# Bank rotation of the last product, tile order of the next layer's first chunk, and a narrower wait of one left part

## The chip, the cores and the metric

The kernel runs on one core of one Trainium2 chip. The metric is device time in microseconds (us) of one execution; three executions of the kernel before are given with their median, and a fourth was profiled.

## What is computed

Two layers of an encoder over 768 tokens (a prompt of 256 and a sample of 512), model width 2048:

```
for l in range(2):
    h = rms_norm(x) * ln_g[l]
    q, k, v, gates = split(h @ w_in[l])
    mix = concat[A(q, k, v) * silu(g_A), B(...) * silu(g_B), C(...) * silu(g_C)]
    x = x + mix @ w_out[l]
```

A, B and C are three kinds of attention (windowed, dense, dilated), and `mix` is 2048 wide. What matters here is the last line, the product of `mix` with `w_out`, and the first line of layer 1, which follows on it.

## The kernel before, in words

**Numbers.** Every fp32 operand is split in a high and a low part (ACT casts the high one, DVE subtracts to get the low one), and each product is three matmuls: high x high, high x low, low x high. The tokens are 6 tiles of 128 (`TT`).

**Stages of a layer.** Input projection (`project_chunk`, 9 slabs of 16 weight chunks, accumulating in banks 0 to 5, one for each token tile; `norm_turns` transposes x beside it, with `norm_hi_parts` on ACT and `norm_lo_parts` on DVE as the evacuation); attention with the gate projection woven in (`gate_piece`); then the output product.

**The output product.** `mix @ w_out` is made as 7 products of half-sized blocks (`PRODUCTS`, Strassen's scheme: 3 token tiles x 2 column slabs each, so 6 tiles, with sums of weights prepared ahead and sums of left parts made on the way). A product is 8 left parts (`KH`) by 2 column slabs (`NH`), 16 chunks; a chunk (`product_step`, L1452 to L1454) is 3 tiles of 3 matmuls. Chunk e of a layer runs from 0 to 111; chunks 96 to 111 are the last product (number 6). Tile b of product p accumulates in bank `out_bank(p, b)`. When a product ends, DVE adds each tile into x (`add_product`, L2162 or L2164), once for each target in `to`: products 0, 2, 3, 4 and 5 have two targets a tile, product 1 and product 6 one. `ADD_AT` puts the adds of tiles 0, 1, 2 in the program at the product's last chunk, those of tiles 3 and 4 one chunk later, tile 5's two later. Before a tile's first matmul PE waits until the adds of all earlier tiles of that bank are done.

**Left parts.** `a_hi_part` (ACT, L1800) and `a_lo_part` (DVE, L2149) write the left operand for part q into a ring of four places. Parts 0 and 1 are made early; part 2 goes to place 0 and part 3 to place 1. These two places lie over the two slots of `gate_t`, in which the gates are kept (gate n of the layer in slot n % 2), so ACT waits for the count `gated`, which POOL raises twice a gate (`gate_product`, L2319). PE needs part q at chunk 2q.

**Queues.** Each engine works off its program in order. In chunk e's turn ACT splits weight chunk e + 4 (L1629; it waits until chunk e - 1 is used), then casts a left part at even e, then does norm work; DVE does adds, the low split of chunk e + 4 (L1890), a sum of left parts (L2142) or a low part (L2149), then norm work. SP issues the DMAs of weights (L1066), of the last mixed chunk's store (L1172), of x (L1218) and of mixed chunks (L1179), in the order of its own program, the loads of x behind the store's landing.

**The way into layer 1.** `NORM_ENTRY` puts the turns of layer 1's first four norm chunks behind chunks 99, 103, 107 and 111 of layer 0, into banks 6 and 7, which the last product leaves free. Then `project_chunk(1, 0)` takes tiles 0 to 5 in banks 0 to 5, each when that bank's adds are done:

```
return (p * OUT_BANKS + b) % 8 if p < N_PROD - 1 else (b + 4) % 6
NORM_ENTRY = {((N_PROD - 1) * KH + 2 * k + 1) * NH + 1: k for k in range(NORM_EARLY)}
act.wait_ge(gated, 2 * (l + 1) * GATE_TILES)
```

Of the kernel before, what the change touches and what calls it, by code (L numbers as in the profile page):

```python
# [31 lines left out]
ACT = mybir.ActivationFunctionType  # L32
# [3 lines left out]
P = 128  # L36
# [4 lines left out]
TT = TOKENS // P  # L41
# [35 lines left out]
KH = KC // 2  # L77
TH = TT // 2
NH = NS_OUT // 2
# [13 lines left out]
OUT_BANKS = TH * NH  # L93
# [2 lines left out]

def out_bank(p, b):

    return (p * OUT_BANKS + b) % 8 if p < N_PROD - 1 else (b + 4) % 6


def quadrant_slab(quadrant, h):
# [289 lines left out]
A_TMP = 3  # L392
A_LEAD = 2

A_EARLY = 2
EARLY_TURN = BIAS_LAST[-1] + 12
NORM_EARLY = KH // 2

NORM_ENTRY = {((N_PROD - 1) * KH + 2 * k + 1) * NH + 1: k for k in range(NORM_EARLY)}
SQUARE_ENTRY = {((N_PROD - 2) * KH + 3) * NH + n + n // 8: divmod(n, TT) for n in range(NH * TT)}  # L400
PER_LOAD = 2
RAW_SLOTS = TT
# [163 lines left out]
def build(nc, x_prompt, x_sample, ln_g, w_in, q_norm_a, k_norm_a, sink_a, q_norm_b, k_norm_b,  # L566
          q_norm_c, k_norm_c, rel_bias, w_out, selector, rope, identity, y_prompt, y_sample):
    with ExitStack() as ctx:
# [150 lines left out]

        bank = [ctx.enter_context(nc.psum_tensor(f"bank{i}", [P, SLAB], F32)) for i in range(8)]  # L720
        acc = bank[0:6]
        turn_bank = bank[6:8]
        s_bank = bank[0:2]
        pt_bank = bank[2:4]
        o_bank = bank[4:6]
# [102 lines left out]
        def turn_evacuated(eng, i):  # L828

            l, s, t, b, _ = TURNS[i]  # L830
            if s == "norm":
                eng.wait_ge(norm_lo, NORM_AT[l, s, t, b] + 1)
            else:
                eng.wait_ge(turned_lo, HEAD_AT[l, s, t] + 1)

        def kv_place(l, u):

# [173 lines left out]
        def turned_parts(l, s, t):  # L1011

            n, nb = HEAD_AT[l, s, t], SLAB_BLOCKS[s] // 2
            src = turn_bank[TURN_AT[l, s, t, 0] % TURN_BANKS][:, 0:nb * P]
            return src, *(turned[:, n % 2, part, 0:nb, :].rearrange("p b c -> p (b c)") for part in range(2))

        def copy_pt(eng, copy, l, i):
# [336 lines left out]
        def _(pe):  # L1354
# [12 lines left out]
            def turn_into(i):  # L1367
                if i >= TURN_BANKS:
                    turn_evacuated(pe, i - TURN_BANKS)
                return turn_bank[i % TURN_BANKS]  # L1370

            def norm_turns(l, k):

                s, j = divmod(k, KC // NS_OUT)
                for g in range(NORM_GROUPS):
                    if l == 0:
                        pe.wait_ge(x_front if k < NORM_LEAD else x_loaded[s], 32)
                    else:
                        pe.wait_ge(out_added, (l - 1) * len(ADDS) + ADDED[s][g])
                        if k == 0 and g == 0:  # L1380
                            for b in (6, 7):
                                pe.wait_ge(out_added, (l - 1) * len(ADDS) + OUT_FREE[b])
                    i = TURN_AT[l, "norm", k, g]
                    dst = turn_into(i)
                    for t in range(NORM_TILES):
                        last = pe.transpose(dst[:, t * P:(t + 1) * P],
                                            x_cols[:, s, g * NORM_TILES + t, j * P:(j + 1) * P], ident[:])
                    last.then_inc(turn_done, 1)
# [13 lines left out]
            def project_chunk(l, c):  # L1402

                s, k = divmod(c, KC)
                n = l * CHUNKS + c
                pe.wait_ge(w_lo_done, n + 1)
                if s == 0:
                    pe.wait_ge(norm_lo, (l * KC + k + 1) * NORM_GROUPS)
                for t in range(TT):
                    if k == 0:  # L1410

                        if n == 0 and t >= ROW_BANK:
                            pe.wait_ge(rows_copied, t - ROW_BANK + 1)
                        if s > 0:
                            pe.wait_ge(acc_copied, (l * NS_IN + s - 1) * TT + t + 1)
                        elif l > 0:
                            pe.wait_ge(out_added, (l - 1) * len(ADDS) + OUT_FREE[t])
                    hi, lo = (tokens_of(a, k, t, s in INTERLEAVED) for a in (act_hi, act_lo))
                    pe.matmul(acc[t][:], hi, w_hi[:, n % W_RING, :], start=(k == 0), stop=False)  # L1419
                    pe.matmul(acc[t][:], hi, w_lo[:, n % W_RING, :], start=False, stop=False)  # L1420
                    last = pe.matmul(acc[t][:], lo, w_hi[:, n % W_RING, :], start=False, stop=(k == KC - 1))  # L1421
                    if k == KC - 1:
                        last.then_inc(acc_done, 1)
                if k < KC - 1:
                    last.then_inc(w_used, 1)
# [195 lines left out]
        def _(act):  # L1621
# [28 lines left out]
            def norm_hi_parts(l, k):  # L1650
                for g in range(NORM_GROUPS):
                    i = TURN_AT[l, "norm", k, g]
                    act.wait_ge(turn_done, i + 1)
                    if i == 0:
                        act.wait_ge(ln_copied, 1)
                    if l > 0 and g == 0:
                        act.wait_ge(a_lo_done, (l - 1) * N_PROD * KH + MIXED_FREE[k])
                    cols = slice(g * NORM_TILES * P, (g + 1) * NORM_TILES * P)
                    nc.scalar.activation(act_hi[:, k, cols], turn_bank[i % TURN_BANKS][:, 0:NORM_TILES * P], ACT.Copy,
                                         scale=ln_cols[:, l * KC + k:l * KC + k + 1]).then_inc(norm_hi, 1)  # L1660

            def drain(l, s, t):
# [123 lines left out]
            def a_hi_part(l, q):  # L1786
                n = l * N_PROD * KH + q
                _, v = a_source(q)
                hi, _ = a_places(q)
                if q < A_EARLY:  # L1790
                    act.wait_ge(early_loaded, 16 * A_EARLY * (l + 1))
                elif PRODUCTS[q // KH]["sign"]:
                    act.wait_ge(a_added, l * a_sums_through(N_PROD * KH - 1) + a_sums_through(q))
                else:
                    a_loaded(act, l, q)
                if q >= A_RING:
                    out_chunk_used(act, l, (q - A_RING) * NH + NH - 1)
                elif q >= A_EARLY:
                    act.wait_ge(gated, 2 * (l + 1) * GATE_TILES)
                nc.scalar.copy(hi, v).then_inc(a_hi_done, 1)  # L1800

            for l in range(DEPTH):
# [64 lines left out]
        def _(dve):  # L1867
# [25 lines left out]
            def norm_lo_parts(l, k):  # L1893
                if l == 0 and k == KC // 2:

                    dve.wait_ge(rows_stored, 16)
                for g in range(NORM_GROUPS):
                    i = TURN_AT[l, "norm", k, g]
                    dve.wait_ge(norm_hi, NORM_AT[l, "norm", k, g] + 1)
                    cols = slice(g * NORM_TILES * P, (g + 1) * NORM_TILES * P)  # L1900
                    nc.vector.scalar_tensor_tensor(
                        out=act_lo[:, k, cols], in0=turn_bank[i % TURN_BANKS][:, 0:NORM_TILES * P],
                        scalar=ln_cols[:, l * KC + k:l * KC + k + 1], in1=act_hi[:, k, cols].bitcast(F32),
                        op0=ALU.mult, op1=ALU.subtract).then_inc(norm_lo, 1)

# [507 lines left out]
```

## Time and profile before

| | |
|---|---|
| three executions | 2830.58, 2831.7, 2842.16 us; median 2831.7 |
| the profiled execution | 2830.3 us, of which the span is 2828.2 |
| mean granted clock | 0.995 |
| busy share of the span | PE 98%, DVE 58%, ACT 43%, POOL 33% |
| chain that ended last | PE 88%, DVE 3%, issue 2%, DMA 2%, POOL 2% |
| layer 0: product stage | 1178 to 1419 us |
| layer 1: product stage | 2583.5 to the end |

Times in the timelines are from the span's start. A row of a timeline gives start, duration, engine, line, operation, output and inputs, and, in brackets, the idle time before it and what released it. A granted clock of 1.00 is TensorE's full 2.4 GHz, 0.50 is 1.2 GHz. Matmuls overlap: their durations are longer than the distance from start to start, which is 0.23 us at full clock for 512 columns, and it is this distance that counts.

### The profile page before, as it was taken

To read this page: it belongs to the slowest core of one execution; us is meant where nothing else is said; L and a number is where in the kernel's file an instruction comes from. 1 tells how busy PE (TensorE), PEld (TensorE's weight loads), DVE (VectorE), ACT (ScalarE), POOL (GpSimd) and SP (SyncE) were. 2 spreads that over 40 slices of the span, in tenths; PEclk is the share of its full clock that TensorE was granted. 3 is DMA by queue.
4 is the path that set the end of the run, shared out by engine and by line. 5 is a ranking of instruction groups with operands and counts; after the bars stand their busy time and mean duration, and the time that the engine had idled before them with its cause. 6 is when DMAs were issued, how large, how long until landed. Compare 5 with 4: busy or idle time off the path is not lost.

```text
span 2828.2 us, 44190 instructions
## 1 busy us (share of the span) xinstructions
PE 2779.0 (98%) x14913; PEld 2493.7 (88%) x14913; DVE 1627.4 (58%) x3973; ACT 1226.1 (43%) x3017; POOL 929.7 (33%) x860
## 2 busy tenths in 40 slices
PE   8999999999999999999999999999999999999998
PEld 7888899988999999888788888999899999998887
DVE  3446644434776677577743465444357766775775
ACT  4322222226665566444542223222266654664443
POOL 0333333310574277400003333333106733774000
PEclk9999999999999999999999999999989999999999
DMA  5366665668444442464525565666684444325645
GB/s 180 110 192 184 186 190 172 187 181 228 134 118 119 126 112 70 150 238 127 193 82 143 170 195 182 184 185 193 178 222 122 112 125 135 89 75 182 211 123 174
DMA packets 420602, 444.25 MB, mean 157 GB/s; under 512 B 62519, under 2 KB 314583, under 8 KB 420380
## 3 DMA queue, kind: packets, MB, share of 16 engines
q1 hardware_dynamic: 420380, 441.44, 52.8%
q8 instruction: 121, 1.98, 0.3%
q14 instruction: 101, 0.83, 0.1%
HBM read 315.54 MB, written 125.80 MB: 156 GB/s over the span
## 4 chain that ended last, share of the span: by engine, by line
PE 88%; DVE 3%; issue 2%; DMA 2%; POOL 2%; ACT 1%; SPq 1%; DVEq 0%; ACTq 0%; POOLq 0%
PE bank L1419 14%; PE bank L1421 14%; PE bank L1420 14%; PE bank L1475 5%; PE bank L1477 5%; PE bank L1476 5%; PE bank L1452 5%; PE bank L1454 5%; PE bank L1453 5%; PE bank L1518 4%; PE bank L1545 2%; PE bank L1504 2%; PE bank L1505 2%; PE bank L1560 1%; PE bank L1561 1%
## 5 line engine op out<-in xcount | busy, mean ns | idle before, releaser
L1890 DVE TENSOR_TENSOR w_lo<-w_raw,w_hi 128x512 fp32r<-128x512 f32 x640 | 455.8, 713 | 473.9 <-ACT w_hi L1629 470.0
L1629 ACT CAST w_hi<-w_raw 128x512 fp32r<-128x512 f32 x640 | 395.5, 619 | 698.7 <-PE bank L1421 410.0
L1419 PE MATMUL bank<-w_hi,act_hi 128*128 128x512 f32 x1728 | 688.8, 399 | 1.4 <-DVE x_cols L2162 1.4
L1421 PE MATMUL bank<-w_hi,act_lo 128*128 128x512 f32 x1728 | 678.6, 393 | 0.0
L1420 PE MATMUL bank<-w_lo,act_hi 128*128 128x512 f32 x1728 | 677.1, 392 | 0.0
L2298 POOL TENSOR_SCALAR prob<-prob,denom 128x256 f32<-128x256 f32 (+2 forms) x288 | 345.1, 1202 | 286.4 <-DVE denom L2021 285.7
L1421 PEld LDWEIGHTS bank<-w_hi,act_lo 128*128 128x128 f32 x1728 | 372.2, 215 | 54.0
L1419 PEld LDWEIGHTS bank<-w_hi,act_hi 128*128 128x128 f32 x1728 | 373.0, 216 | 51.8 <-DVE x_cols L2162 1.9
L1420 PEld LDWEIGHTS bank<-w_lo,act_hi 128*128 128x128 f32 x1728 | 373.0, 216 | 48.6
L1475 PE MATMUL bank<-act_hi,w_hi 128*128 128x384 f32 x1024 | 347.5, 339 | 0.0
L1477 PE MATMUL bank<-act_hi,w_lo 128*128 128x384 f32 x1024 | 345.7, 338 | 0.0
L1476 PE MATMUL bank<-act_lo,w_hi 128*128 128x384 f32 x1024 | 345.4, 337 | 0.0
L1452 PE MATMUL bank<-w_hi,a_part 128*128 128x512 f32 x672 | 265.2, 395 | 12.9 <-DVE x_cols L2162 8.0
L1453 PE MATMUL bank<-w_lo,a_part 128*128 128x512 f32 x672 | 263.0, 391 | 0.0
L1454 PE MATMUL bank<-w_hi,a_part 128*128 128x512 f32 x672 | 262.8, 391 | 0.0
L2289 POOL TENSOR_TENSOR y<-y,gains 128x256 f32<-128x256 f32 (+1 forms) x144 | 159.9, 1122 | 266.6 <-DVE y L1923 266.6
L2012 DVE TENSOR_TENSOR pt_lo<-bank,pt_hi 128x256 fp32r<-128x256 f32 (+2 forms) x288 | 153.4, 533 | 129.0 <-ACT pt_hi L1726 125.9
L1956 DVE TENSOR_TENSOR turned<-bank,turned 128x512 fp32r<-128x512 f32 (+1 forms) x96 | 63.2, 658 | 276.9 <-ACT turned L1696 276.8
L1726 ACT CAST pt_hi<-bank 128x256 fp32r<-128x256 f32 (+2 forms) x288 | 132.9, 461 | 187.2 <-PE bank L1518 180.0
L1696 ACT CAST turned<-bank 128x512 fp32r<-128x512 f32 (+1 forms) x96 | 53.7, 560 | 364.7 <-PE bank L1399 360.4
L1518 PE MATMUL bank<-ident,prob 128*128 128x128 f32 x1232 | 207.7, 275 | 2.5 <-POOL prob L2298 2.5
L1476 PEld LDWEIGHTS bank<-act_lo,w_hi 128*128 128x128 f32 x1024 | 193.1, 189 | 4.2
(121 smaller groups left out, 4651.3 us busy)
## 6 DMA issues: line engine op xcount, KB each, us to landing
w_raw<-w_in SPq DMA_DIRECT2D x144, 512.0 KB, 4.6
w_sums<-sum_out SPq DMA_DIRECT2D x32, 1280.0 KB, 6.6
w_raw<-w_sums SPq DMA_DIRECT2D x80, 512.0 KB, 4.1
sum_in<-w_out SPq DMA_DIRECT2D x64, 512.0 KB, 5.6
heads_t<-turned SPq DMA_DIRECT2D x240, 128.0 KB, 2.4
q_t<-heads_t SPq DMA_DIRECT2D x192, 128.0 KB, 2.1
k_t<-keys_t SPq DMA_DIRECT2D x48, 384.0 KB, 5.6
w_raw<-w_out SPq DMA_DIRECT2D x32, 512.0 KB, 3.8
```

The source lines that it names most:

```text
L1419: pe.matmul(acc[t][:], hi, w_hi[:, n % W_RING, :], start=(k == 0), stop=False)
L1420: pe.matmul(acc[t][:], hi, w_lo[:, n % W_RING, :], start=False, stop=False)
L1421: last = pe.matmul(acc[t][:], lo, w_hi[:, n % W_RING, :], start=False, stop=(k == KC - 1))
L1452: pe.matmul(bank[at][:], hi[:, tokens], w_hi[:, n % W_RING, :], start=(j == 0), stop=False)
L1453: pe.matmul(bank[at][:], hi[:, tokens], w_lo[:, n % W_RING, :], start=False, stop=False)
L1454: last = pe.matmul(bank[at][:], lo[:, tokens], w_hi[:, n % W_RING, :], start=False, stop=(j == KH - 1))
L1475: pe.matmul(out, hi, act_hi[:, k, tokens], start=(k == 0), stop=False)
L1476: pe.matmul(out, hi, act_lo[:, k, tokens], start=False, stop=False)
L1477: last = pe.matmul(out, lo, act_hi[:, k, tokens], start=False, stop=(k == KC - 1))
L1629: nc.scalar.copy(w_hi[:, n % W_RING, :], w_raw[:, load % W_RAW, j, :]).then_inc(w_hi_done, 1)
L1890: nc.vector.tensor_tensor(w_lo[:, n % W_RING, :], w_raw[:, load % W_RAW, j, :], w_hi[:, n % W_RING, :].bitcast(F32), ALU.subtract).then_in ...
L2298: nc.gpsimd.tensor_scalar(v, v, denom[:, pair % STAT_SLOTS, st["r"]:st["r"] + 1], None, ALU.mult)\
```

## The change

Three edits. The last product's tiles take the next six of all eight banks like the other products (4, 5, 6, 7, 0, 1); banks 2 and 3 are left over (`SPARE_BANK`). The first four norm turns of layer 1 go to these two banks, and behind chunks 103, 105, 107 and 109; the following ones go to banks 6 and 7 as before, the first of them with a wait for those banks' adds. Layer 1's first chunk takes its tiles in the order 4, 5, 2, 3, 0, 1, with a wait for the norm evacuation at tiles 2 and 3. And ACT's wait before left part 2 asks for 15 gates of the layer rather than 16; before part 3 it stays 16.

```
 def out_bank(p, b):
-    return (p * OUT_BANKS + b) % 8 if p < N_PROD - 1 else (b + 4) % 6
+    return (p * OUT_BANKS + b) % 8
+
+SPARE_BANK = min(set(range(8)) - {out_bank(N_PROD - 1, b) for b in range(OUT_BANKS)})
...
+NEXT_ORDER = (4, 5, 2, 3, 0, 1)
-NORM_ENTRY = {((N_PROD - 1) * KH + 2 * k + 1) * NH + 1: k for k in range(NORM_EARLY)}
+NORM_ENTRY = {((N_PROD - 1) * KH + k + 3) * NH + 1: k for k in range(NORM_EARLY)}
...
+        def turn_place(i):
+            l, s, k, _, _ = TURNS[i]
+            return bank[(SPARE_BANK if l > 0 and s == "norm" and k < NORM_EARLY else 6) + i % TURN_BANKS]
...
-                        if k == 0 and g == 0:
-                            for b in (6, 7):
+                        if k in (0, NORM_EARLY) and g == 0:
+                            for b in (SPARE_BANK, SPARE_BANK + 1) if k == 0 else (6, 7):
                                 pe.wait_ge(out_added, (l - 1) * len(ADDS) + OUT_FREE[b])
...
-                for t in range(TT):
+                for t in NEXT_ORDER if l > 0 and c == 0 else range(TT):
...
                             pe.wait_ge(out_added, (l - 1) * len(ADDS) + OUT_FREE[t])
+                            if t in (SPARE_BANK, SPARE_BANK + 1):
+                                pe.wait_ge(norm_lo, NORM_AT[l, "norm", NORM_EARLY - 1, NORM_GROUPS - 1] + 1)
...
                 elif q >= A_EARLY:
-                    act.wait_ge(gated, 2 * (l + 1) * GATE_TILES)
+                    act.wait_ge(gated, 2 * ((l + 1) * GATE_TILES - (A_RING - 1 - q)))
```

## Rows read from the trace of the kernel before

**Rows 1.** The page's first part: busy time and share of the span.

```profile
PE 2779.0 (98%) x14913; PEld 2493.7 (88%) x14913; DVE 1627.4 (58%) x3973; ACT 1226.1 (43%) x3017; POOL 929.7 (33%) x860
```

**Rows 2.** PE's waits: waited for, us in all, times, longest.

```profile
PE bank L1452 <- DVE x_cols L2162: 8.0, 10, 1.4
```

**Rows 3.** PE's timeline, layer 0, first chunks of the last product.

```profile
1379.95 0.39 PE L1452 MATMUL bank<-w_hi,a_part 128*128 128x512 f32 x1
...
1383.93 0.47 PE L1452 MATMUL bank<-w_hi,a_part 128*128 128x512 f32 x1 [1.40 <-DVE x_cols L2162]
...
1388.11 0.40 PE L1452 MATMUL bank<-w_hi,a_part 128*128 128x512 f32 x1
```

**Rows 4.** DVE's timeline, the same stretch.

```profile
1377.85 3.67 DVE L2162 TENSOR_TENSOR x_cols<-bank,x_cols 128x512 f32<-128x512 f32 x6
...
1382.51 2.47 DVE L2162 TENSOR_TENSOR x_cols<-bank,x_cols 128x512 f32<-128x512 f32 x4
```

**Rows 5.** PE's timeline, chunk 65 of layer 0.

```profile
1315.87 0.39 PE L1452 MATMUL bank<-w_hi,a_part 128*128 128x512 f32 x1
...
1318.55 0.40 PE L1452 MATMUL bank<-w_hi,a_part 128*128 128x512 f32 x1
```

**Rows 6.** PE's timeline where layer 1 begins.

```profile
1419.32 0.48 PE L1419 MATMUL bank<-w_hi,act_hi 128*128 128x512 f32 x1
...
1421.68 0.50 PE L1419 MATMUL bank<-w_hi,act_hi 128*128 128x512 f32 x1 [1.42 <-DVE x_cols L2162]
```

**Rows 7.** DVE's timeline where layer 1 begins.

```profile
1419.89 1.14 DVE L1901 SCALAR_TENSOR_TENSOR act_lo<-bank,ln_cols,act_hi 128x384 fp32r<-128x384 f32 x2 [1.24 <-ACT act_hi L1659]
...
1420.95 1.87 DVE L2162 TENSOR_TENSOR x_cols<-bank,x_cols 128x512 f32<-128x512 f32 x3
```

**Rows 8.** PE's timeline, chunks 3 to 6 of layer 0.

```profile
1186.01 0.39 PE L1454 MATMUL bank<-w_hi,a_part 128*128 128x512 f32 x1
...
1188.41 0.47 PE L1452 MATMUL bank<-w_hi,a_part 128*128 128x512 f32 x1 [2.02 <-DVE a_part L2149]
...
1194.21 0.40 PE L1452 MATMUL bank<-w_hi,a_part 128*128 128x512 f32 x1
```

**Rows 9.** Stretches: busy time of each engine, PEclk, DMA share, GB/s.

```profile
1188.00:1192.00 4.00, 3.59 (x10) 2.88 (x11) 2.54 (x5) 1.46 (x4) 0.00 (x0) 0.63 0.78 214
...
2594.00:2599.00 5.00, 5.00 (x15) 3.98 (x16) 3.19 (x6) 1.57 (x4) 0.00 (x0) 0.66 0.88 275
...
2080.00:2097.00 17.00, 17.00 (x79) 16.80 (x78) 6.58 (x36) 7.78 (x36) 0.00 (x0) 0.50 0.77 193
```

**Rows 10.** ACT's timeline, layer 0, around the wait for the last gate.

```profile
1180.92 1.12 ACT L1629 CAST w_hi<-w_raw 128x512 fp32r<-128x512 f32 x2
...
1186.04 0.51 ACT L1800 CAST a_part<-act_hi 128x384 fp32r<-128x384 f32 x1 [3.99 <-POOL mixed_t L2319]
```

**Rows 11.** POOL's timeline, layer 0: products of gates 14 and 15.

```profile
1167.22 2.00 POOL L2319 TENSOR_TENSOR mixed_t<-mixed_t,gate_t 128x384 f32<-128x384 f32 x2
...
1183.51 1.47 POOL L2319 TENSOR_TENSOR mixed_t<-mixed_t,gate_t 128x384 f32<-128x384 f32 x1
```

**Rows 12.** DVE's timeline, layer 0: the low split of chunk 4.

```profile
1182.59 1.50 DVE L1890 TENSOR_TENSOR w_lo<-w_raw,w_hi 128x512 fp32r<-128x512 f32 x1
```

**Rows 13.** A stretch of layer 1 behind chunk 10, columns as in rows 9.

```profile
2612.00:2616.00 4.00, 4.00 (x19) 3.31 (x18) 1.39 (x3) 1.56 (x3) 0.00 (x0) 1.00 1.03 417
```

**Rows 14.** ACT's waits, layer 1, 2592 to 2630 us, columns as in rows 2.

```profile
ACT w_hi L1629 <- DMA w_raw<-w_sums: 8.7, 4, 3.2
```

**Rows 15.** PE's timeline, chunk 17 of layer 1, third tile.

```profile
2624.91 0.50 PE L1452 MATMUL bank<-w_hi,a_part 128*128 128x512 f32 x1 [1.24 <-DVE x_cols L2162]
```

**Rows 16.** SP's timeline, layer 0: the store of the last mixed chunk.

```profile
1188.18 0.43 SPq L1172 DMA_DIRECT2D mix_rows<-mixed_t  x1
```

**Rows 17.** One line's instructions (probability turns): durations, first and last start; both layers.

```profile
L1518 PE MATMUL bank<-ident,prob x616: 270/272/421, 655.1 to 1174.4; 128*128 128x128 f32 x154
...
L1518 PE MATMUL bank<-ident,prob x616: 270/272/435, 2057.9 to 2579.9; 128*128 128x128 f32 x154
```

More of the change, by code:

```diff
@@ L97, in out_bank @@
 def out_bank(p, b):
-    return (p * OUT_BANKS + b) % 8 if p < N_PROD - 1 else (b + 4) % 6
+    return (p * OUT_BANKS + b) % 8
+SPARE_BANK = min(set(range(8)) - {out_bank(N_PROD - 1, b) for b in range(OUT_BANKS)})
+assert SPARE_BANK + 1 not in {out_bank(N_PROD - 1, b) for b in range(OUT_BANKS)}
 def quadrant_slab(quadrant, h):
@@ L721, in build @@
         acc = bank[0:6]
-        turn_bank = bank[6:8]
         s_bank = bank[0:2]
@@ L1013, in turned_parts @@
             n, nb = HEAD_AT[l, s, t], SLAB_BLOCKS[s] // 2
-            src = turn_bank[TURN_AT[l, s, t, 0] % TURN_BANKS][:, 0:nb * P]
+            src = turn_place(TURN_AT[l, s, t, 0])[:, 0:nb * P]
             return src, *(turned[:, n % 2, part, 0:nb, :].rearrange("p b c -> p (b c)") for part in range(2))
@@ L1369, in turn_into @@
                     turn_evacuated(pe, i - TURN_BANKS)
-                return turn_bank[i % TURN_BANKS]
+                return turn_place(i)
             def norm_turns(l, k):
@@ L1658, in norm_hi_parts @@
                     cols = slice(g * NORM_TILES * P, (g + 1) * NORM_TILES * P)
-                    nc.scalar.activation(act_hi[:, k, cols], turn_bank[i % TURN_BANKS][:, 0:NORM_TILES * P], ACT.Copy,
+                    nc.scalar.activation(act_hi[:, k, cols], turn_place(i)[:, 0:NORM_TILES * P], ACT.Copy,
                                          scale=ln_cols[:, l * KC + k:l * KC + k + 1]).then_inc(norm_hi, 1)
@@ L1901, in norm_lo_parts @@
                     nc.vector.scalar_tensor_tensor(
-                        out=act_lo[:, k, cols], in0=turn_bank[i % TURN_BANKS][:, 0:NORM_TILES * P],
+                        out=act_lo[:, k, cols], in0=turn_place(i)[:, 0:NORM_TILES * P],
                         scalar=ln_cols[:, l * KC + k:l * KC + k + 1], in1=act_hi[:, k, cols].bitcast(F32),
```

## The prediction

> **What bounds the kernel now.** I read four views: the page, PE's waits, the timelines around each stall, and the stretches. TensorE (PE) is busy 98% of the span [rows 1], so only a pause of PE, or a matmul at the low clock, is worth time. PE's longest entry in the product stage are banks not yet added out, 8.0 us in 10 waits [rows 2]; its timeline adds a wait of 2.02 us for a part of the left operand, once a layer [rows 8], and one where layer 1 begins [rows 6].
>
> Call e the product chunks: 112 a layer, 16 a product, nine matmuls in three tiles each. Undisturbed chunks take 2.05 us, a tile 0.68.
>
> **Part 1, the last product's banks.** Chunk 96 starts at 1379.95, chunk 98 at 1388.11: 8.16 us for two chunks worth 4.09 [rows 3]. Product 6 takes banks 4, 5, 0, 1, 2, 3. Banks 0 to 3 hold product 5's tiles 2 to 5, and each of those needs two adds of 0.6 us; DVE ends the tenth add at about 1385.0 and the last two at 1387.2 [rows 4], and PE waits for bank 3. After the change the order is 4, 5, 6, 7, 0, 1: tile 2 needs two adds (done 1379.1), tile 3 four (1380.3), tile 4 six (1381.5), and only tile 5 meets an add that is late, as it needs product 5's tile 3 (1383.8 where PE asks at 1383.36). Earlier boundaries have that pattern where the product in front has two targets and the one behind makes sums, as here. Chunk 65 is one: 1315.87 to 1318.55, 2.68 us [rows 5]. So the two chunks take 2.05 + 2.68 = 4.73 instead of 8.16: 3.4 us. Layer 1 has the same boundary: **6.9 us**. Added instructions: none. DVE does the same adds in the same order, and chunk 98, now at 1384.7, finds its weights and left part ready; chunk 100 (1388.8) needs a left part that DVE finishes near 1388.3, so 0.5 us of cover is left there.
>
> **Part 2, where layer 1 begins.** PE starts tile 0 at 1419.32, tile 1 only at 1421.68 [rows 6], 1.58 us late, and the tile behind the pause is 0.12 longer. Bank 1's add stood in DVE's queue behind the norm evacuation of chunk 3, turned only after chunk 111 (1419.89, 2 x 0.53), and began at 1420.95 [rows 7]. After the change that turn comes after chunk 109, and the first chunk takes banks 4, 5 (added out long before), 2, 3 (the norm turns' banks, evacuated by then), 0, 1. Bank 0 is asked for four tiles in, 2.7 us after the start; its add can end about 1 us after it. Four turn pairs are issued before and after, so nothing is paid. They now stand two chunks apart instead of four: 4.1 us plus the turn, against about 2 us from a turn to its evacuation, so ACT and DVE keep up. The added waits (spare banks at the first turn, banks 6 and 7 at the fifth, the norm evacuation at tiles 2, 3) ask for work finished 2 us or more before; behind them stands all of PE's queue, so a late one would cost its full lateness. **1.7 us.**
>
> **Part 3, the third left part.** PE finishes chunk 3 at 1186.24 and starts chunk 4 at 1188.41, and chunk 6 at 1194.21 [rows 8]. Chunks 4 and 5 took 5.80 us for 4.09: the granted clock fell behind the pause, 0.63 over 1188 to 1192 and 0.66 in layer 1 [rows 9], that is, matmuls at 1.2 GHz, 0.43 us apart for 0.23. ACT waits 3.99 us for the last gate product before it casts this part (1186.04) [rows 10]; its own gates were done at 1169.2 [rows 11]. After the change ACT casts it behind the splits of chunks 3 and 4, at 1182.0 [rows 10], and splits chunks 5 and 6 until 1183.5, then waits for the last gate with the fourth part, which PE needs only at chunk 6 (about 1191.4); what queues behind that wait on ACT are the splits of chunks 7 and 8, needed later still.
>
> Next late is DVE. Its queue is split 3, split 4 (to 1184.09), split 5, low part, and POOL's last two products run beside them. Rows: a split that takes 0.69 alone took 1.50 there, and a POOL product that takes 1.0 took 1.47 [rows 11, 12]. Those lengths fit turns: POOL's first product ends at 1184.98, 0.9 after split 4. With turns, split 5 runs 1185.0 to 1185.6, POOL's second product 1185.6 to 1186.6, the low part (a quarter shorter than a split, 0.5) to 1187.1, and PE starts chunk 4 at 1187.2. Bounds: with no disturbance at all the part is ready at 1185.3 and PE never waits (1186.24); with the old order it stays 1188.41. I take 1187.2, since the rows beside it show exactly such neighbours. The Trainium skill's page "SBUF — State Buffer", section "Who interferes with whom", says a VectorE instruction with two SBUF inputs and a GpSimd one exclude each other for the whole instruction, not by a share of bandwidth. By that rule the wait left is the 1 us above; by a mere stretching of DVE's work (1.50 for 0.69) PE would start near 1186.5, and the sum would be 1.4 us larger.
>
> So the pause shrinks from 2.2 to about 1 us, 1.2 saved, and behind so short a pause I expect no fall of the clock, as none followed the 1.4 us pauses of part 1 [rows 3] and part 2 [rows 6]: 5.80 less 4.09 and 0.1 for the restart, 1.6 more. Twice 2.8: **5.6 us.**
>
> **What is given back.** Right behind, 1198 to 1215 in layer 0 and 2604 to 2624 in layer 1, all 16 DMA engines are full (share 1.03 [rows 13]): weights, x and mixed chunks. In layer 1 ACT already waits 8.7 us for weights [rows 14]; DVE's adds for product 0 queue behind that split, and chunk 17's third tile waits until 2624.91 [rows 15], 0.9 us more than chunk 65's pattern. The change brings PE 2.8 us forward there, but these transfers hang on the store of the last mixed chunk (1188.18 [rows 16]), which waits for POOL and comes only 1.5 us sooner. The weights are then 1.3 us later against PE: 1.3 us lost in layer 1. In layer 0 ACT never waited for weights; I take 0.2, between nothing and 1.3. Bounds: nothing, or all of layer 1's 2.8. **Minus 1.5 us.**
>
> **Sum.** 6.9 + 1.7 + 5.6 - 1.5 = 12.7 us from the profiled execution's 2830.3: **2817.6 us**. Its span is 2828.2, 2.1 lie around it, unchanged. It stands 1.4 under the median of 2831.7.
>
> **The rivals.**
> A. The faster side: DVE and POOL do not take turns, and the transfers give nothing back. Then part 3 is worth 3.8 a layer (2.2 + 1.6), and the sum is 16.2: 2814.1. For it: a weight has several chunks of lead before PE itself lacks it. Against it: rows 12, 15.
>
> B. The low clock is not the pause's doing, or comes anyway: 3.2 less, 2820.8. For it: one pause of 1.4 us drew no fall and one of 2 did, so the border is close, and the split pauses of part 1 summed to 4 without one. Against it: it came in both layers at the same chunk. The Trainium skill's page "TensorE: Matmul & The Clock Gate", section "Why this matters for your kernels", has the clock fall only behind an idle gap longer than any pause of these product stages. By that rule the falls at chunk 4 would have another cause and stay; the trace speaks against it, 2.2 us were enough twice.
>
> C. The transfers take back all that part 3 gains in layer 1, at chunk 17: 1.5 more lost, and with it some of layer 0's, 2820.
>
> D. Layer 1's attention keeps its clock. In the profiled execution PE ran 17 us at 0.50 there [rows 9], and from the first to the last probability turn its attention took 2.7 us longer than layer 0's [rows 17]. With everything shifted by 10 us it may go either way: 2814.9 if it vanishes.
>
> E. Slower. One mechanism: the enlarged wait at layer 1's chunk 17 drops the clock, and it stays low through product 1. A chunk at 1.2 GHz costs 3.84 us for 2.05. It turns the sign behind 7 such chunks (12.7 / 1.8) and passes the border of measurement behind 15; 16 give 2846.4. Against it: low stretches in the product stages lasted one short spell and ended by themselves.
>
> F. The change does not do what it says: a wait for the spare banks or the norm evacuation sits as long as the old one, and parts 1 and 2 give nothing in one layer: 2822.
>
> **How the numbers follow.** Forecast 0.50, A 0.15, B 0.12, C 0.09, D 0.08, E 0.03, F 0.03. About 0.5% (14 us) is what a measurement can tell from no change. The forecast lies 14.1 us under the median of 2831.7, right on that border, but 12.7 against its own execution; of its 0.50 I count 0.22 as faster. Faster: 0.22 + A 0.15 + D 0.08 = 0.45. Same: 0.28 + 0.12 + 0.09 + 0.03 = 0.52. Slower: 0.03. The range: down to A with D's 2.7 (2811), up to B plus C's 1.5 and the 1.4 between execution and median (2824).
>
> **What would show it.** Chunks 96 and 97 together at 4.7 us in both layers; no PE pause in layer 1's first chunk, tiles in banks 4, 5, 2, 3, 0, 1; chunk 4 starting about 1 us behind chunk 3 and chunks 4, 5 at 4.2 us with the clock at 1.00; the low part's cast by ACT near 1182; chunk 17 of layer 1 longer than 3.58. Wrong would be: the clock still 0.6 at chunk 4 (B), chunk 4 with no wait (A), chunk 17 unchanged, or attention's stretches moving by more than 3 us, which nothing in this change does on purpose.

## The result and the profile after

In the same rounds the kernel before took 2838.38 us (median of 6, 2830.58 to 2842.99) and the changed one 2820.26 us (median of 6, 2819.92 to 2829.08): ratio 0.9946, 95% interval 0.9924 to 0.9968. The change is faster, clear of noise; whether by more than the prediction's own border of 0.5% (0.995) is not settled, since that border lies inside the interval. The profiled execution took 2819.95 us, its span is 2817.8, against 2828.2 before. The medians lie 18.1 us apart and the two profiles 10.3, while the places that the change touches account for 12.7; what is left on either side is of the size by which attention differs from execution to execution (below).

The table follows the prediction's sum, from landmark to landmark in the two traces (start of a chunk to start of a chunk, in us, minus is faster). "Give-back" is what the change loses again at product 0's end:

| | predicted | measured |
|---|---|---|
| Part 1, chunks 96 and 97, two layers | -6.9 | -3.46, -3.46 |
| Part 2, chunk 98 to layer 1's second chunk | -1.7 | -1.75 |
| Part 3, pause ahead of chunk 4, two layers | -2.4 | -1.45, -1.45 |
| Part 3, clock in chunks 4 and 5, two layers | -3.2 | -1.60, -1.61 |
| give-back, chunks 16 and 17, layer 0 / layer 1 | +0.2 / +1.3 | +1.51 / +0.54 |
| sum of the change | -12.7 | -12.7 |
| start and layer 0's attention | 0 | -2.4 |
| layer 1's attention | 0 | +4.9 |

PE's totals, the page's first part:

```profile
PE 2775.1 (98%) x14913; PEld 2493.4 (88%) x14913; DVE 1631.1 (58%) x3973; ACT 1226.3 (44%) x3017; POOL 931.8 (33%) x860
```

PE's waits in the product stages (us in all, times, longest): the waits for banks of [rows 2] fell from 8.0 to 4.3 us, and the left part's 2.02 a layer became 0.56. (L1465 is the old L1452, L2175 and L2177 the old L2162 and L2164, L2162 the old L2149.)

```profile
PE bank L1465 <- DVE x_cols L2175: 4.3, 8, 1.3
PE bank L1465 <- DVE a_part L2162: 1.1, 2, 0.6
PE bank L1465 <- DVE x_cols L2177: 0.7, 2, 0.3
```

PE's timeline, first the two chunks at the last product's begin (answer to [rows 3]), then chunks 3, 4 and 6 (answer to [rows 8]):

```profile
1375.95 0.39 PE L1465 MATMUL bank<-w_hi,a_part 128*128 128x512 f32 x1
...
1379.86 0.50 PE L1465 MATMUL bank<-w_hi,a_part 128*128 128x512 f32 x1 [0.34 <-DVE x_cols L2175]
...
1380.65 0.40 PE L1465 MATMUL bank<-w_hi,a_part 128*128 128x512 f32 x1
...
1181.82 0.39 PE L1465 MATMUL bank<-w_hi,a_part 128*128 128x512 f32 x1
...
1184.58 0.47 PE L1465 MATMUL bank<-w_hi,a_part 128*128 128x512 f32 x1 [0.56 <-DVE a_part L2162]
...
1188.78 0.39 PE L1465 MATMUL bank<-w_hi,a_part 128*128 128x512 f32 x1
```

Chunks 96 and 97 take 4.70 us, with one wait of 0.34 in the last tile, where the prediction had it. Chunk 4 waits 0.56, and it and chunk 5 then take 4.20. The granted clock behind both pauses, in a view of stretches (columns as in [rows 9]), is 1.00 where it was 0.63 and 0.66:

```profile
1184.00:1189.00 5.00, 4.43 (x20) 3.68 (x20) 3.96 (x7) 2.59 (x5) 0.02 (x1) 1.00 0.92 280
2588.00:2593.00 5.00, 4.82 (x21) 4.06 (x22) 3.56 (x7) 2.69 (x6) 0.00 (x0) 1.00 0.89 280
```

In layer 1's first chunk (answer to [rows 6]) tiles stand 0.68 apart, with no pause; its second chunk begins at 1416.62, behind a norm turn:

```profile
1411.95 0.39 PE L1432 MATMUL bank<-w_hi,act_hi 128*128 128x512 f32 x1
...
1412.63 0.39 PE L1432 MATMUL bank<-w_hi,act_hi 128*128 128x512 f32 x1
...
1415.36 0.39 PE L1432 MATMUL bank<-w_hi,act_hi 128*128 128x512 f32 x1
...
1416.62 0.48 PE L1432 MATMUL bank<-w_hi,act_hi 128*128 128x512 f32 x1
```

What was given back shows at chunk 17 of layer 0. ACT's timeline, DVE's and PE's:

```profile
1203.65 0.62 ACT L1642 CAST w_hi<-w_raw 128x512 fp32r<-128x512 f32 x1 [3.84 <-DMA w_raw<-w_sums]
...
1208.60 3.67 DVE L2175 TENSOR_TENSOR x_cols<-bank,x_cols 128x512 f32<-128x512 f32 x6
...
1214.59 0.50 PE L1465 MATMUL bank<-w_hi,a_part 128*128 128x512 f32 x1 [1.31 <-DVE x_cols L2175]
```

ACT waits 3.84 us for one weight chunk and 1.66 us for the next, so DVE's queue runs late, and the six adds of product 0 begin only 0.58 us ahead of chunk 16 (1209.18). At chunk 64, undisturbed, they begin 2.1 us ahead (1307.79 for 1309.88). So PE waits 1.31 us for a bank at chunk 17, which lasts 4.16 us for 2.65 before. Before, ACT's waits in layer 0 name no weight transfer from 1184 to 1219 us.

### The profile page after: what moved, and what is told of

It reads as the page before. It is cut to its first block, busy times and chain, and to the rows that moved or that the text cites. A ratio compares the mean times of both kernels' runs of the same rounds, so it can differ in the third digit from the quotient of the medians.

```text
span 2817.8 us, 44193 instructions
## 1 busy us (share of the span) xinstructions
PE 2775.1 (98%) x14913; PEld 2493.4 (88%) x14913; DVE 1631.1 (58%) x3973; ACT 1226.3 (44%) x3017; POOL 931.8 (33%) x860
## 4 chain that ended last, share of the span: by engine, by line
PE 87%; DVE 4%; ACT 2%; issue 2%; POOL 2%; DMA 2%; SPq 0%; DVEq 0%; ACTq 0%; POOLq 0%
PE bank L1434 14%; PE bank L1432 14%; PE bank L1433 14%; PE bank L1488 5%; PE bank L1490 5%; PE bank L1489 5%; PE bank L1465 4%; PE bank L1467 4%; PE bank L1466 4%; PE bank L1531 4%; PE bank L1558 2%; PE bank L1517 2%; PE bank L1518 2%; PE bank L1573 1%; PE bank L1574 1%
## 5 line engine op out<-in xcount | busy, mean ns | idle before, releaser
L1465 PE MATMUL bank<-w_hi,a_part 128*128 128x512 f32 x672 | 263.7, 392 | 6.1 <-DVE x_cols L2175 4.3
L2302 POOL TENSOR_TENSOR y<-y,gains 128x256 f32<-128x256 f32 (+1 forms) x144 | 159.9, 1123 | 266.0 <-DVE y L1936 266.0
```

The source lines that it names most:

```text
L1465: pe.matmul(bank[at][:], hi[:, tokens], w_hi[:, n % W_RING, :], start=(j == 0), stop=False)
```

## The experiments

All but the last start from the changed kernel. Numbers 1 to 6, 8 and 12 are one execution each, so of these the totals say little and the landmarks count. "Chunk 4's pause" is what lies between chunk 3's start and chunk 4's beyond 2.05 us; gains are given from start to start.

**1. The rotation alone.** The gate wait, the turns' places and the tile order go back.

```
-NORM_ENTRY = {((N_PROD - 1) * KH + k + 3) * NH + 1: k ...}
+NORM_ENTRY = {((N_PROD - 1) * KH + 2 * k + 1) * NH + 1: k ...}
...
-                for t in NEXT_ORDER if l > 0 and c == 0 else range(TT):
+                for t in range(TT):
...
-                    act.wait_ge(gated, 2 * ((l + 1) * GATE_TILES - (A_RING - 1 - q)))
+                    act.wait_ge(gated, 2 * (l + 1) * GATE_TILES)
```

> The changed kernel with the old turn places in the program (behind chunks 99, 103, 107, 111), the old tile order 0 to 5 and the old wait for all 16 gates: only the banks are rotated, with the norm turns in the spare banks. Theory: the rotation is worth its 3.4 us a layer by itself, chunks 96 and 97 together 4.7 us; chunk 4 is back at 4.2 us late start and low clock (chunks 3 to 5 together 10.0 us); and the way into layer 1 gets worse than before, since bank 0 now holds the last product's tile 4: from the start of chunk 111 to the second chunk of layer 1 about 10.3 us, where before had 9.1. Rival: the way into layer 1 is bounded by the norm evacuation alone and stays at 9.1.

2832.27 us, span 2830.1. Chunks 96 and 97 keep their 4.70 us, so part 1 is the rotation's alone. Chunk 4's pause is back (2.2 us), the low clock too (chunks 4 and 5: 5.79 and 5.76), and chunk 17 is back to 2.67 and 2.84. The way from chunk 111 to layer 1's second chunk takes 13.33 us, against 6.70 in the changed kernel and 9.12 before, more than either theory said. PE's timeline, DVE's, and the stretch behind:

```profile
1420.92 0.77 PE L1432 MATMUL bank<-w_hi,act_hi 128*128 128x512 f32 x1 [2.81 <-DVE x_cols L2175]
```

```profile
1418.44 1.14 DVE L1914 SCALAR_TENSOR_TENSOR act_lo<-bank,ln_cols,act_hi 128x384 fp32r<-128x384 f32 x2 [1.24 <-ACT act_hi L1672]
1419.50 1.88 DVE L2175 TENSOR_TENSOR x_cols<-bank,x_cols 128x512 f32<-128x512 f32 x3
```

```profile
1418.00:1425.00 7.00, 4.19 (x12) 3.24 (x11) 3.53 (x6) 1.39 (x3) 0.00 (x0) 0.66 0.60 207
```

Tile 0 asks for bank 0, which after the rotation holds the last product's tile 4, whose add is the second of the three that DVE has behind the norm evacuation: 2.81 us of pause. The matmuls behind it run at the low clock, the first five tiles 1.3 to 1.4 us apart. From chunk 98 to the second chunk it is 4.2 us slower than before. The rotation is paid for only together with the new tile order.

**2. The old places of the turns**, with rotation and tile order kept.

```
-NORM_ENTRY = {((N_PROD - 1) * KH + k + 3) * NH + 1: k ...}
+NORM_ENTRY = {((N_PROD - 1) * KH + 2 * k + 1) * NH + 1: k ...}
```

> The changed kernel with only the norm turns back behind chunks 99, 103, 107, 111; the tile order 4, 5, 2, 3, 0, 1 stays. Theory: most of part 2 comes from the order. The third tile (bank 2) waits some 0.4 us for the fourth norm evacuation; from the start of chunk 111 to the second chunk of layer 1 7.7 us, against 6.7 in the changed kernel, of which 0.57 is the turn that now stands in this stretch. Rival: DVE's adds behind that evacuation decide, as they did before, and the stretch is 9.1 us.

2827.75 us. The way from chunk 111 takes 7.89 us, one turn of 0.57 us more in it and small waits, the longest at tile 2 for the norm evacuation (0.24 us idle). From chunk 98 on, where both have the same four turns, it is 0.5 us longer than the changed kernel's. So of part 2's 1.75 us, 1.24 are the tile order with the banks, and 0.5 the turns' places. Most of the 7.5 us to the changed kernel's median lies ahead of the product stages: layer 0's attention took 6.4 us longer.

**3. The third left part waits for all gates again.**

```
-                    act.wait_ge(gated, 2 * ((l + 1) * GATE_TILES - (A_RING - 1 - q)))
+                    act.wait_ge(gated, 2 * (l + 1) * GATE_TILES)
```

> The changed kernel with the third part again waiting for all 16 gates. Theory: chunk 4 starts 4.2 us after chunk 3 in both layers (2.76 in the changed kernel), the clock falls behind that pause in both layers and chunks 4 and 5 together take 5.8 us; chunk 17 goes back to 2.65 us in layer 0 and to about 3 in layer 1 (4.16 and 4.12 in the changed kernel). In all 4 us longer in the two product stages. Rival (B of the prediction): the low clock has another cause; then it stays away here as it does in the changed kernel, and chunks 4 and 5 take 4.2 us behind the same pause.

2817.01 us, less than the changed kernel, since layer 1's attention took 8.0 us less. Where the edit is, chunk 4's pause is back in both layers (+1.45). But the clock fell behind it only in layer 1 (chunk 4: 3.65 us). In layer 0 the pause is as long, and the clock stays:

```profile
1187.00:1192.00 5.00, 4.36 (x19) 3.67 (x20) 3.93 (x8) 2.32 (x5) 0.00 (x0) 1.00 0.73 231
```

So the fall at this place does not follow from the pause each time. And where the clock stayed, chunks 16 and 17 took 2.23 + 4.18 us; where it fell, 2.04 + 2.68. What the clock takes at chunk 4, chunk 17 gives back.

**4. The last gate product cut to 8 of its 384 columns** in each half, so the other 376 columns of that mixed chunk stay ungated. This takes POOL's last work out of DVE's way.

```
+                if n == GATE_TILES - 1:
+                    tokens = slice(h * HALF, h * HALF + 8)
```

> The changed kernel in which POOL multiplies only 8 of 384 columns of each half for the last gate of a layer (the other columns of that chunk stay without their gate). Theory: DVE's split of chunk 5 and the third low part are late because POOL's two last products stand between them; without these each takes 0.7 and 0.55 us, and chunk 4 starts 2.05 to 2.1 us after chunk 3 in both layers (2.76 in the changed kernel). Rival: they are late for weights or for ACT; then chunk 4 stays at 2.7.

2817.12 us. Chunk 4 starts with no wait in both layers (-0.72), so the pause left comes from POOL's last products standing beside DVE's queue. Chunks 16 and 17 together become longer, by 0.63 us in layer 0 and 1.02 in layer 1.

**5. The low part ahead of the split** on DVE, for chunk 4's left part only.

```
+                    if e == 1:
+                        a_lo_part(l, A_LEAD)
                     for c in out_splits(e):
...
-                    if h == 1 and q + A_LEAD < N_PROD * KH:
+                    if h == 1 and e > 1 and q + A_LEAD < N_PROD * KH:
```

> The changed kernel in which DVE makes the third low part before the low split of chunk 5, not behind it. Theory: what PE waits for at chunk 4 is DVE's and POOL's turns; the part is now one turn earlier, ends 1.3 us sooner, and chunk 4 starts 2.05 to 2.1 us after chunk 3 in both layers (2.76 in the changed kernel): 0.7 us a layer. Chunk 5's split still ends about 1 us before PE asks. Rival: the split then comes too late and chunk 5 takes over the wait.

2819.16 us. The same 0.72 without leaving work out, and about 0.1 more in chunks 4 and 5. Chunks 16 and 17 take it back and more: +2.03 us in layer 0 and +1.03 in layer 1.

**6. The mixed chunks loaded four left parts later.**

```
-                    if 5 <= q < 5 + KH // 2:
+                    if 9 <= q < 9 + KH // 2:
...
```

> The changed kernel with the loads of the second eight mixed chunks issued four left parts later (from part 9 on instead of 5; they are first needed for part 16). Theory: chunk 17 is long because these loads and the loads of x fill the DMA engines, the weights land late and DVE's adds queue behind a split; with the loads out of the way chunk 17 takes 2.65 us in both layers (4.16 and 4.12 in the changed kernel), 1.5 us a layer, and ACT waits for no weights between chunks 8 and 22. Rival: the loads of x alone are to blame and chunk 17 stays above 3.5; or the later loads meet the x loads of parts 13 and 14 and the same loss shows at chunk 33 or 49.

2818.09 us. Chunk 17 took 3.73 and 4.11 us, so moving the mixed chunks does not free it. They have a part in it all the same: chunk 18 began 1.1 us sooner behind the last landing of x than in the changed kernel, but that landing itself came 0.6 and 1.1 us later (21.16 and 21.57 us behind chunk 3's start, for 20.55 and 20.44).

**7. Both, the low part first and the mixed chunks later.**

> The changed kernel with both: the third low part before the split of chunk 5, and the mixed loads four parts later. Theory: 0.7 and 1.5 us a layer add up to 4.4 us; about 2815.6 us where attention runs as in the changed kernel's faster executions (2820), ratio to before 0.993. Rival: less than 1 us together, since what the transfers gave back is taken elsewhere.

2818.66 us (median of 7, 2816.73 to 2826.97), ratio to before 0.9960 [0.9945, 0.9976]. About 0.8 us a layer is gained at chunks 3 to 5, and chunk 17 stays at 4.01 and 4.16. From chunk 3 to chunk 18 the two layers are 1.7 us shorter together, where the theory had 4.4.

**8. The loads of x spread out.** Slab 0 one left part later, slab 1 three.

```
-                    if q in (3, 4, 13, 14):
-                        load_x(l, (3, 4, 13, 14).index(q))
+                    if q in (4, 6, 13, 14):
+                        load_x(l, (4, 6, 13, 14).index(q))
```

> The changed kernel with only the two early loads of x moved: slab 0 one left part later, slab 1 three parts later, so that the four transfers are issued over about 8 us instead of 2.4 us. Theory: what is given back at chunks 16 and 17 comes from the x transfers, which go out in one burst just as the weights of chunks 17 to 20 are wanted; spread out, they let the weights land earlier, DVE reaches its adds for product 0 sooner, and chunks 16 and 17 together take at most 5.4 us in both layers instead of 6.2 (about 0.8 to 1.5 us gained a layer). Rival 1: it is the sum of bytes (x and mixed chunks) between the end of attention and chunk 16; moving a part of them inside that stretch does nothing, and the two chunks stay at 6.0 us or more. Rival 2: slab 1 now lands too late for its own adds, and chunks 17 and 18 become longer than before. Total by the theory about 2817 to 2819, apart from what attention does by itself.

2821.85 us in one execution, with 170.9 us of attention in layer 1. Chunks 16 and 17 together take 4.70 and 4.72 us, as chunks 64 and 65 do in every kernel: 1.50 and 1.44 us gained. ACT's waits around chunk 17 of layer 0, first the changed kernel (1182 to 1216 us), then this one (1185 to 1219):

```profile
ACT w_hi L1642 <- DMA w_raw<-w_sums: 10.6, 5, 3.8
```

```profile
ACT w_hi L1642 <- DMA w_raw<-w_sums: 3.6, 2, 2.8
```

and this kernel's adds and PE's wait at chunk 17 (it begins at 1214.38, chunk 18 at 1217.03):

```profile
1210.23 3.67 DVE L2175 TENSOR_TENSOR x_cols<-bank,x_cols 128x512 f32<-128x512 f32 x6
...
1216.23 0.50 PE L1465 MATMUL bank<-w_hi,a_part 128*128 128x512 f32 x1 [0.34 <-DVE x_cols L2175]
```

The adds begin 2.1 us ahead of chunk 16 again. SP's timeline shows the burst of x in the changed kernel, and in this one two loads at a time, with weights between them:

```profile
1188.01 0.38 SPq L1229 DMA_DIRECT2D x_cols<-x_prompt  x1
1188.43 0.47 SPq L1229 DMA_DIRECT2D x_cols<-x_sample  x1
1188.95 0.50 SPq L1077 DMA_DIRECT2D w_raw<-w_sums  x1
1189.49 0.84 SPq L1229 DMA_DIRECT2D x_cols<-x_prompt  x1
1190.37 1.38 SPq L1229 DMA_DIRECT2D x_cols<-x_sample  x1
1192.40 0.43 SPq L1077 DMA_DIRECT2D w_raw<-w_sums  x1
```

```profile
1191.88 0.44 SPq L1229 DMA_DIRECT2D x_cols<-x_prompt  x1
1192.36 0.47 SPq L1229 DMA_DIRECT2D x_cols<-x_sample  x1
1195.54 0.34 SPq L1077 DMA_DIRECT2D w_raw<-w_sums  x1
...
1199.99 0.43 SPq L1229 DMA_DIRECT2D x_cols<-x_prompt  x1
1200.46 0.47 SPq L1229 DMA_DIRECT2D x_cols<-x_sample  x1
```

In the changed kernel the weight chunk issued at 1192.40, behind all four, landed at 1203.62, 1.26 us after the last of x.

**9. All three: x spread, mixed chunks later, low part first.**

> The changed kernel with x spread as in the run before, the mixed chunks loaded four parts later, and the low part ahead of DVE's split at chunk 4. Theory (bytes in front of chunk 16 are what delays the weights): chunk 4 starts without a wait (0.7 us gained a layer) and chunks 16 and 17 together take 4.7 to 5.2 us in both layers, as at the later product boundaries, so 1.0 to 1.5 us more a layer; together 3.5 to 4.4 us less than the changed kernel outside attention. Rival (chunk 17 is late for another reason than transfers, e.g. DVE's own queue): the two chunks stay at 6 us, and only the 1.6 us of chunk 4 are gained, or nothing. Total by the theory about 2816, with attention moving it by several us either way.

2817.57 us (median of 5, 2809.76 to 2822.12), ratio to before 0.9955 [0.9941, 0.9968]. Chunk 4 has no wait (-0.72, and -0.1 behind it), chunk 17 takes 2.66 in both layers; together 2.3 us a layer less than the changed kernel, 4.6 in all, a little more than the 3.5 to 4.4 expected.

**10 and 11. Two controls, nothing edited:** the changed kernel again, and number 9 again beside it.

> The changed kernel once more, nothing edited. Theory (the low clock in attention comes and goes from execution to execution, whatever the edits): the product stages repeat to 0.05 us (chunk 3 at 2.76, chunk 17 at 4.16 and 4.12, chunk 97 at 2.66), but the way from the first to the 200th probability turn of either layer differs from the first profile of this kernel by 2 us or more in at least one layer. Rival (the attention time belongs to the program: an edit shifts it by altering the phase, and it repeats): both attention stages repeat to 0.5 us, and the differences of 2 to 9 us between kernels are each kernel's own.

> The kernel with x spread, the mixed chunks later and the low part first, once more, on the same chip and beside the changed kernel. Its product stages are 4.5 us shorter than the changed kernel's (0.84 + 1.48 a layer) and should repeat to 0.1 us. Theory: with the low clock in attention coming and going, its median lies 3 to 6 us under the changed kernel's in the same rounds. Rival: attention takes back what the product stages give, as after a shift of phase, and the medians lie within 1.5 us.

The changed kernel: 2822.69 us (median of 7, 2813.38 to 2827.89). Number 9: 2812.36 (median of 6, 2810.05 to 2818.16), ratio to before 0.9924 [0.9907, 0.9941]. Over all their executions the medians are 2820.42 (13) and 2815.06 (11), 5.4 us apart; in these rounds alone they are 10.3 apart, where 3 to 6 were expected. In the product stages number 9 is 4.6 us ahead of the changed kernel's first profile and 2.8 of its second; no profile shows where the rest of the 10.3 lies, and attention's spread is of that size. By its median number 9 is ahead of both kernels.

The expectation for the changed kernel failed twice. Chunk 17 took 3.23 and 3.18 us, not 4.16 and 4.12: the last of x landed 1 us sooner behind chunk 3 in this execution. And its attention differed by 1.8 and 1.5 us from its first profile, between what theory and rival said. Number 9's two profiles differ by 5.2 us in layer 0's attention and by 0.3 in layer 1's.

**12. The kernel before, again.**

> The kernel before once more, nothing edited. Theory (the edited places are the program's, the low clock in attention and the transfers' landing belong to the execution): chunks 3 and 96 to 97 repeat (4.22 us, and 8.16 us for the two), the way into layer 1 repeats to 0.05 us; the clock falls behind the 2 us pause at chunk 4 in most but not surely in both layers (chunks 4 and 5 either 5.8 or 4.2 us); chunk 17 lies between 2.65 and 4.2 us in either layer; attention differs by 2 us or more in at least one layer. Rival: chunk 4, chunk 17 and attention repeat to 0.1 us, and so the chunk 17 of the changed kernel is its own property.

2826.34 us. Chunks 96 and 97 and the way into layer 1 repeat to 0.01 us. In layer 1 the pause at chunk 4 is there (2.01 us), and the clock stays at 1.00:

```profile
2590.03 0.47 PE L1452 MATMUL bank<-w_hi,a_part 128*128 128x512 f32 x1 [2.01 <-DVE a_part L2149]
```

```profile
2590.00:2594.00 4.00, 3.97 (x18) 3.33 (x19) 3.15 (x6) 1.71 (x4) 0.00 (x0) 1.00 0.90 242
```

There chunks 16 and 17 took 7.26 us, 1.64 more than in the first profile of this kernel, where the clock had cost 1.62 at chunk 4.

## Why the prediction was right, and where it was not

The prediction was right: 2817.6 us was forecast and 2820.26 measured, inside the range of 2811 to 2824. Parts 1 and 2 were right by their own steps, and so was the pause of part 3, to 0.25 us a layer. The clock's share and what was given back were counted apart, though they hang together, and there luck helped.

**Part 1** came out to 0.02 us. The order of the adds and the counts by tile decided it, read off chunk 65, and experiment 1 shows it to be the rotation's alone.

**Part 2** came out too. What the prediction did not say is how much the rotation needs the tile order: without it the way into layer 1 becomes 4.2 us slower than before. The added waits cost nothing seen at their places; the evacuation wait bites only with the turns in their old places (0.24 us).

**Part 3, the pause.** 1.45 us were saved for 1.2. ACT cast the part at 1179.58, where the forecast 1182.0, less the 2.4 us that this stage began sooner, has 1179.6. The low part ended 0.42 us behind PE's last matmul of chunk 3, where 0.86 was forecast. DVE's timeline (then the same two kinds of instruction where POOL is idle) and POOL's:

```profile
1179.18 1.11 DVE L1903 TENSOR_TENSOR w_lo<-w_raw,w_hi 128x512 fp32r<-128x512 f32 x1 [2.35 <-ACT w_hi L1642]
1180.21 1.50 DVE L1903 TENSOR_TENSOR w_lo<-w_raw,w_hi 128x512 fp32r<-128x512 f32 x1
1181.64 1.51 DVE L1903 TENSOR_TENSOR w_lo<-w_raw,w_hi 128x512 fp32r<-128x512 f32 x1
1183.07 1.37 DVE L2162 TENSOR_TENSOR a_part<-act_hi,a_part 128x384 fp32r<-128x384 f32 x1
...
1212.19 0.68 DVE L1903 TENSOR_TENSOR w_lo<-w_raw,w_hi 128x512 fp32r<-128x512 f32 x1
1212.79 0.55 DVE L2162 TENSOR_TENSOR a_part<-a_sum,a_part 128x384 fp32r<-128x384 f32 x1
```

```profile
1179.82 1.34 POOL L2321 TENSOR_TENSOR gate_t<-gate_t,tanh_t 128x384 f32<-128x384 f32 x1
1181.13 1.47 POOL L2332 TENSOR_TENSOR mixed_t<-mixed_t,gate_t 128x384 f32<-128x384 f32 x1
1182.55 1.47 POOL L2332 TENSOR_TENSOR mixed_t<-mixed_t,gate_t 128x384 f32<-128x384 f32 x1
```

The ends alternate strictly. DVE's first three come at 1180.29, 1181.71 and 1183.15, POOL's at 1181.16, 1182.60 and 1184.02, and each engine's next end is 1.4 us behind its last. Alone a split takes 0.6 us from start to start (1212.19 to 1212.79) and a POOL product 1.0 [rows 11], so a step is somewhat less than one of each, 1.6. Had both engines only been slowed side by side, DVE's shorter instructions would have ended more often than POOL's. So the rows fit turns, as the prediction took them, and not stretching. Experiment 4 cuts the last two POOL products short, and the wait is gone. The Trainium skill's page "SBUF — State Buffer", section "Who interferes with whom", has the two exclude each other for a whole instruction; these rows agree.

**Part 3, the clock.** Right in the trace, and too sure in the prediction. Count all profiles by the pause ahead of chunk 4: behind 2.0 us (before and its control, experiments 1 and 3) the clock fell in 6 of 8 layers; behind 0.6 us (the changed kernel twice, experiments 2, 6 and 8) in none of 10; with no pause (4, 5, 7, 9 and 11) in none of 10. So rival B falls: the fall at chunk 4 comes with the long pause and not without it. The Trainium skill's page "TensorE: Matmul & The Clock Gate", section "Why this matters for your kernels", warns only of gaps longer than any of these pauses, and the runs do not agree that shorter ones are safe: 2.0 us were enough 6 times in 8. But the 1.6 us were not all there to be won: where the clock stays up, PE reaches chunk 16 that much earlier and waits there (experiments 3 and 12). The control of the kernel before shows it best: from chunk 3 to chunk 18 layer 1 took 36.02 us with the clock down and 36.04 with the clock up. With x loaded at its old places, the clock's 3.2 us and the give-back are one account, and the prediction had them as two.

**What was given back** is the term that failed. 1.5 us were forecast, 0.2 in layer 0 and 1.3 in layer 1; measured were 1.5 and 0.5 in the first profile of the changed kernel, and 0.6 and, a gain, -0.4 in the second. So 2.05 us in one execution and 0.2 in another, for 1.5: the sum was near by luck.

The step that failed was "in layer 0 ACT never waited for weights; I take 0.2": the view showed that nothing waited, not how close it was. The burst of x fixes the time instead. In 11 layers in which chunk 17 was long with the loads at their old places (both kernels, their controls, experiments 1, 2, 4 and 5), chunk 18 began 13.01 to 13.10 us after the last transfer of x had landed; with the mixed chunks later (6, 7) 11.93 to 11.97. In layer 0 of experiments 3 to 5 it was 14.05 to 14.21. The second weight chunk behind x accounts for both: it landed 4.47 to 4.55 us after x in the 11 layers and 5.50 to 5.66 in those three, and in all 14 chunk 18 began 8.54 to 8.56 us after it. Why it came 1 us later in the three is open.

Counted from chunk 3, PE came 3.05 us sooner to chunk 16 than before. The prediction had the transfers 1.5 us sooner. The last of x landed 0.5 us sooner in layer 0 (20.55 for 21.07, from chunk 3's start), where 1.0 us of slack had been left (14.06 for 13.05), and 2.5 us sooner in layer 1 (20.44 for 22.95), which had none: 3.05 - 0.5 - 1.0 and 3.05 - 2.5 are the 1.5 and the 0.5. Experiment 8 undoes it by the places of x alone, in both layers; the six layers with x spread have chunk 17 at 2.66 to 2.68, the 14 with an early chunk 4 and x at the old places at 3.18 to 4.18.

The rows of DVE's queue behind the second weight chunk, which landed at 1206.84 in layer 0 of the changed kernel, show where the 8.5 us go:

```profile
1207.52 0.69 DVE L1903 TENSOR_TENSOR w_lo<-w_raw,w_hi 128x512 fp32r<-128x512 f32 x1 [0.98 <-ACT w_hi L1642]
1208.13 0.55 DVE L2155 TENSOR_TENSOR a_sum<-act_hi 128x384 f32<-128x384 f32 x1
```

ACT casts it at 1206.87, DVE splits it, makes a sum of left parts, and then works without a pause through the six adds, a split and a low part to the add that PE waits for at 1214.59. Which of these could be moved out of the way was not tried. Rival C had the mechanism, and put the larger loss in the wrong layer.

**Attention** moved by more than 3 us, as the prediction said nothing in this change does on purpose. The first 200 probability turns took 159.9 to 171.0 us over 28 layers (two in each of the 14 profiles). What differs are stretches at the low clock, as in [rows 9]: where the mean grant over these turns was 0.99 they took 159.9 to 162.3 us, and where it was 0.92, 170.9 and 171.0. The mean grant of the stretch of layer 1 is 0.94 in the changed kernel and 0.99 in experiment 9:

```profile
2048.00:2220.00 172.00, 165.68 (x1143) 162.48 (x1143) 113.39 (x511) 109.29 (x384) 71.28 (x69) 0.94 0.57 153
```

```profile
2048.00:2220.00 172.00, 165.85 (x1192) 162.41 (x1191) 117.55 (x526) 113.85 (x395) 75.72 (x74) 0.99 0.60 159
```

One kernel, nothing edited, differs by 3.6 us (before, layer 1) and 5.2 (experiment 9, layer 0) between two profiles. Whether a kernel also has its own share in it is not settled: layer 1 of the changed kernel took 169.5 and 171.0, of experiment 9 162.3 and 162.6. This spread is as large as the 0.5% border, and so the class of a change of 12.7 us was, as forecast, near a toss. Rival D went the other way: 4.9 us more, not 2.7 less. Of the others, A falls with the turns and with chunk 17, F with parts 1 and 2, and E with the granted clock, which stayed at 1.00 over chunk 17 in both layers (1209 to 1216 and 2614 to 2620 us). What makes attention's stretches come and go was not tried.

## What to carry to other kernels

When a pause is removed, look for the next place where the engine meets something that did not move with it (here x's transfers, 13 chunks on), and count how early it now comes, not whether it waited before. Loads that nobody needs for 20 us should not go out in one burst ahead of the weights that the next chunks need: moving the two early loads of x in SP's program won 1.4 to 1.5 us a layer against the changed kernel's first profile (chunk 17 at 2.66 to 2.68 us in all six layers that had it). And a rotation of buffers has to be followed by its readers' order; alone it cost 4.2 us at the next stage's first tile. For differences of 0.2% compare landmarks in the traces, stage by stage, since totals of single executions put experiment 3, which is 3.3 us slower in its product stages by its edit, ahead of the kernel that it was made from.

## What was not expected of the hardware

The clock's fall is not a function of the pause alone: the same wait of 2.0 us, in the same place of the same program, drew 1.2 GHz for some 3 us in one profile (chunks 4 and 5: 5.78 us) and nothing in the next (4.16 us). And the landing of the same transfers, the first issued 6.2 and 6.5 us behind chunk 3's start, differed by 0.9 us between two executions (20.55 and 19.62 us after chunk 3's start), which PE passed on in full at chunk 17 (4.16 and 3.23).
